# A convolution and squared-ReLU MLP layer on one core: five staging places for the spilled operands, their transfers issued by ScalarE

## The reference, cut to what matters

```python
h = rmsnorm(x, mix_norm[0])
b_gate, c_gate, v = jnp.split(h @ w_in, 3, axis=-1)      # 2048 -> 3 x 2048
u = c_gate * v
y = (b_gate * causal_conv3(u, conv_w)) @ w_out
x = x + y
h2 = rmsnorm(x, mlp_norm[0])
a = jax.nn.relu(h2 @ mlp_w1)                             # 2048 -> 8192
x = x + (a * a) @ mlp_w2                                 # 8192 -> 2048
```

## Time and profile before

| what | value |
|---|---|
| median of three runs | 2052.66 us |
| the profiled execution | 2047.96 us |
| its span, first to last instruction | 2046.2 us |
| TensorE busy (matmuls, pipelined) | 1978.9 us, 97% |
| VectorE busy | 1481.7 us, 72% |
| ScalarE busy | 851.3 us, 42% |
| GpSimd busy | 75.6 us, 4% |
| spills: 112 transfers of 512 KB from GpSimd's queue | median 7.0 us from issue to landing |

### The profile page before, as it was taken

The page is one execution under the profiler, slowest core; times in us unless marked ns, Lnnn a source line. Parts: engine busy times, 40 slices in busy tenths (PEclk is TensorE's granted clock), DMA queues, the critical chain, the costliest instruction groups (busy, mean ns, idle before and its releaser), DMA issues. The chain is left out here.

```text
span 2046.2 us, 22931 instructions
## 1 busy us (share of the span) xinstructions
PE 1978.9 (97%) x8778; PEld 1623.0 (79%) x8778; DVE 1481.7 (72%) x1368; ACT 851.3 (42%) x1002; POOL 75.6 (4%) x146
## 2 busy tenths in 40 slices
PE   8999999999999999999998999998999999999999
PEld 7888888888887877777777777777788888888887
DVE  6345363353535499879897988989888979978878
ACT  6222222222234465555545555554444433433332
POOL 0000000000000110100101010010000000000000
PEclk9999999999999999999999999999999999999999
DMA  5322222222223544757667476769889878878783
GB/s 186 118 88 103 103 82 103 102 89 95 100 98 123 196 185 165 280 211 305 242 237 276 176 274 236 285 236 367 324 318 379 330 304 325 322 308 323 273 318 134
DMA packets 98317, 445.92 MB, mean 218 GB/s; under 512 B 10800, under 2 KB 10800, under 8 KB 73776
## 3 DMA queue, kind: packets, MB, share of 16 engines
q1 hardware_dynamic: 78944, 375.42, 49.4%
q0 software_dynamic: 19136, 69.21, 8.4%
q10 hardware_dynamic: 144, 0.04, 0.0%
HBM read 371.24 MB, written 73.40 MB: 217 GB/s over the span
## 5 line engine op out<-in xcount | busy, mean ns | idle before, releaser
L1073 PE MATMUL pair<-ring,act 128*128 128x512 f32 x5376 | 1246.8, 392 | 28.5 <-DVE ring L788 18.3
L1073 PEld LDWEIGHTS pair<-ring,act 128*128 128x128 f32 x5376 | 1009.3, 189 | 251.9 <-issue 39.9
L451 ACT ACTIVATE ring<-raw 128x1024 fp32r<-128x1024 f32 x448 | 466.1, 1056 | 582.6 <-PE pair L1073 350.3
L788 DVE TENSOR_TENSOR ring<-raw,ring 128x1024 fp32r<-128x1024 f32 x448 | 540.3, 1221 | 122.2 <-ACT ring L451 120.6
L590 DVE TENSOR_TENSOR w_lo<-w_raw,w_hi 128x512 fp32r<-128x512 f32 x256 | 175.7, 692 | 348.4 <-ACT w_hi L374 343.2
L374 ACT ACTIVATE w_hi<-w_raw 128x512 fp32r<-128x512 f32 x256 | 161.4, 631 | 474.4 <-PE pair L978 471.8
L978 PE MATMUL pair<-h_hi,w_lo 128*128 128x512 f32 x764 | 297.8, 390 | 0.0
L978 PE MATMUL pair<-h_hi,w_hi 128*128 128x512 f32 x764 | 297.2, 389 | 0.0
L978 PE MATMUL pair<-h_lo,w_hi 128*128 128x512 f32 x764 | 297.2, 389 | 0.0
L783 DVE TENSOR_TENSOR raw<-raw 128x2048 f32<-128x2048 f32 x128 | 292.8, 2288 | 5.6
L978 PEld LDWEIGHTS pair<-h_hi,w_lo 128*128 128x128 f32 x764 | 143.4, 188 | 30.6 <-issue 0.8
(11 more groups left out here) (78 smaller groups left out, 750.6 us busy)
## 6 DMA issues: line engine op xcount, KB each, us to landing
raw<-in_mlp SPq DMA_DIRECT2D x128, 1024.0 KB, 7.6
act<-spill SPq DMA_DIRECT2D x224, 512.0 KB, 6.3
w_raw<-in_weights SPq DMA_DIRECT2D x63, 1024.0 KB, 4.9
spill<-stage POOLq DMA_DIRECT2D x112, 512.0 KB, 7.0
act<-act_kept SPq DMA_DIRECT2D x84, 512.0 KB, 7.6
act_kept<-act POOLq DMA_DIRECT2D x12, 512.0 KB, 6.3
mixed<-turned POOLq DMA_DIRECT2D x16, 256.0 KB, 2.9
x<-mixed SPq DMA_DIRECT2D x8, 512.0 KB, 12.7
```

The lines of the kernel that those rows point to most:

```text
L451: nc.scalar.activation(ring[g % RING][:, 0], raw[:, r, 2 * (s % 2):2 * (s % 2) + 2, :], ACT.Copy).then_inc(hi_ready, 1)
L788: nc.vector.tensor_tensor(ring[g % RING][:, 1], raw[:, RAW_OF[s // 2], 2 * (s % 2):2 * (s % 2) + 2, :], ring[g % RING][:, 0].bitcast(F32), ...
L1073: mm = nc.tensor.matmul(bank, stationary, moving, start=(opens and k == 0 and n == 0), stop=(closes and k == NT - 1 and n == 2))
```

## The change

The staging places become five (four at RESID + 16 to 32 KB, the fifth at TMP). The order of the spills and the slots in which they are split and formed change. Each pair of transfers is issued by ScalarE, in the slot after its split, behind that slot's other work, instead of by GpSimd. To make room, the sum for the first product moves to U_PAD (over quad L12) and that for L22 to H_LO + 28 KB (over quad L21), and the waits of `copy_product` and `copy_first` change with them; the waits for `turn_out` at v = 0 remain only before the copy of the fourth product. Other places in RESID are renumbered.

```diff
-SPILLS = (L11, L12, L22, S1, S3, S2, S4)
+SPILLS = (L11, L22, L12, S1, S3, S2, S4)
-SPLIT_AT = {(0, 5): 0, (0, 8): 1, (0, 9): 2, (0, 11): 3, (0, 13): 4, (1, 1): 5, (1, 3): 6}
-FORM_AT = {(0, 10): (0, 1), (0, 12): (2,), (1, 2): (3,)}
+SPLIT_AT = {(0, 4): 0, (0, 6): 1, (0, 8): 2, (0, 10): 3, (0, 12): 4, (1, 0): 5, (1, 3): 6}
+FORM_AT = {(0, 9): (0, 1), (0, 12): (2,), (1, 1): (3,)}
+STAGES = 5
...
-        sums = [at(f"sum{n}", RESID + 4 * KB * n, [P, 2, BW]) for n in range(6)]
-        q_first, q_s1, q_s2, q_s3, q_s4, q_l22 = sums
-        second_s1 = at("second_s1", RESID, [P, NT, HALF])
+        q_s1, q_s2, q_s3, q_s4 = (at(f"sum{n}", RESID + 4 * KB * n, [P, 2, BW]) for n in range(4))
+        q_first = at("sum_first", U_PAD, [P, 2, BW])
+        q_l22 = at("sum_l22", H_LO + 28 * KB, [P, 2, BW])
+        second_s1 = at("second_s1", RESID + 16 * KB, [P, NT, HALF])
...
-        stage = [at("stage0", RESID + 24 * KB, [P, NT, HALF], F32R), at("stage1", RESID + 28 * KB, [P, NT, HALF], F32R),
-                 at("stage2", TMP, [P, NT, HALF], F32R)]
+        stage = [at(f"stage{i}", a, [P, NT, HALF], F32R)
+                 for i, a in enumerate([RESID + (16 + 4 * i) * KB for i in range(4)] + [TMP])]
...
@@ gpsimd
-            def put_spill(c, n):
-                for half in range(2):
-                    w = 2 * (NPROD * c + n) + half
-                    pool.wait_ge((stage_hi, stage_lo)[half], NPROD * c + n + 1)
-                    pool.dma_start(spill[c, SPILLS[n], half], stage[w % 3][:].bitcast(F32)).then_inc(spilled[w % 3], 16)
...
-            for c in range(NC):
-                for n in range(NPROD):
-                    put_spill(c, n)
@@ scalar, copy_product(v, i)
-                if q == 0:
-                    act.wait_ge(turned, KT)
-                    act.wait_ge(turn_out, 16 * KT)
-                elif i in (0, 3, 4):
-                    act.wait_ge(quad_turned, 4 * (q - 1) + {0: 2, 3: 3, 4: 4}[i])
+                if i == 4:
+                    if q == 0:
+                        act.wait_ge(act_lo_ready, NPROD + SECOND.index(S3) + 1)
+                    else:
+                        act.wait_ge(stage_lo, NPROD * (q - 1) + SPILLS.index(S3) + 1)
+                elif q == 0:
+                    act.wait_ge(turned, 3 * NT)
+                    if i == 3:
+                        act.wait_ge(turn_out, 16 * KT)
+                elif i in (0, 3):
+                    act.wait_ge(quad_turned, 4 * (q - 1) + {0: 2, 3: 3}[i])
@@ copy_first(q)
-                    act.wait_ge(quad_turned, 4 * (q - 1) + 1)
+                    act.wait_ge(stage_lo, NPROD * q)
                 else:
-                    act.wait_ge(act_lo_ready, NPROD + SECOND.index(S2) + 1)
+                    act.wait_ge(act_lo_ready, NPROD + SECOND.index(S4) + 1)
@@ new on scalar
+            def put_spill(c, n):
+                for half in range(2):
+                    w = 2 * (NPROD * c + n) + half
+                    act.wait_ge((stage_hi, stage_lo)[half], NPROD * c + n + 1)
+                    act.dma_start(spill[c, SPILLS[n], half],
+                                  stage[w % STAGES][:].bitcast(F32)).then_inc(spilled[w % STAGES], 16)
...
                     if 2 <= v < UP and (v % 2, s) in SPLIT_AT:
                         split_z_hi(q - 1, SPLIT_AT[v % 2, s])
+                    if 2 <= v < UP and (v % 2, s - 1) in SPLIT_AT:
+                        put_spill(q - 1, SPLIT_AT[v % 2, s - 1])
                     if v >= UP and (v - UP, s) in LATE:
                         split_z_hi(NC - 1, LATE[v - UP, s])
+                    if v >= UP and (v - UP, s - 1) in LATE:
+                        put_spill(NC - 1, LATE[v - UP, s - 1])
```

More of the change, by code:

```diff
@@ L123, in conv_mlp_layer @@
         quad = {"L11": quads1[:, 0], "L21": quads1[:, 1], "L12": quads2[:, 0], "L22": quads2[:, 1]}
-        sums = [at(f"sum{n}", RESID + 4 * KB * n, [P, 2, BW]) for n in range(6)]
-        q_first, q_s1, q_s2, q_s3, q_s4, q_l22 = sums
-        second_s1 = at("second_s1", RESID, [P, NT, HALF])
-        turned_out = [at("turned0", RSTD, [P, BW])] + [at(f"turned{i + 1}", RESID + (16 + 2 * i) * KB, [P, BW])
-                                                        for i in range(4)]
-        stage = [at("stage0", RESID + 24 * KB, [P, NT, HALF], F32R), at("stage1", RESID + 28 * KB, [P, NT, HALF], F32R),
-                 at("stage2", TMP, [P, NT, HALF], F32R)]
+        q_s1, q_s2, q_s3, q_s4 = (at(f"sum{n}", RESID + 4 * KB * n, [P, 2, BW]) for n in range(4))
+        q_first = at("sum_first", U_PAD, [P, 2, BW])
+        q_l22 = at("sum_l22", H_LO + 28 * KB, [P, 2, BW])
+        second_s1 = at("second_s1", RESID + 16 * KB, [P, NT, HALF])
+        turned_out = [at("turned0", RSTD, [P, BW])] + [at(f"turned{i + 1}", RESID + a * KB, [P, BW])
+                                                        for i, a in enumerate((12, 14, 20, 22))]
+        stage = [at(f"stage{i}", a, [P, NT, HALF], F32R)
+                 for i, a in enumerate([RESID + (16 + 4 * i) * KB for i in range(4)] + [TMP])]
         acts1 = [at(f"act{j}", H_HI + 8 * KB * j, [P, 2, NT, HALF], F32R) for j in range(NPROD)]
@@ L138, in conv_mlp_layer @@
         x11, x21, x22, x12 = (at(f"x{q}", Z_LO + 8 * KB * n, [P, NP, 2, BW]) for n, q in enumerate(("11", "21", "22", "12")))
-        sum_s1 = [at("sum_s1_0", RESID + 8 * KB, [P, 2, BW]), at("sum_s1_1", RESID + 12 * KB, [P, 2, BW])]
-        sum_s2 = [at("sum_s2_0", RESID, [P, 2, BW]), at("sum_s2_1", RESID + 4 * KB, [P, 2, BW])]
+        sum_s1 = [at("sum_s1_0", RESID + 4 * KB, [P, 2, BW]), at("sum_s1_1", RESID + 8 * KB, [P, 2, BW])]
+        sum_s2 = [at("sum_s2_0", RESID, [P, 2, BW]), at("sum_s2_1", RESID + 12 * KB, [P, 2, BW])]
         pairs = [ctx.enter_context(nc.psum_tensor(f"pair{i}", [P, 2, BW], F32)) for i in range(NT)]
@@ L188, in conv_mlp_layer @@
         stage_lo = sem("stage_lo")
-        spilled = [sem(f"spilled{i}") for i in range(3)]
+        spilled = [sem(f"spilled{i}") for i in range(STAGES)]
         raw_turn_in = [sem(f"raw_turn_in{i}") for i in range(4)]
@@ L210, in spills_done @@
             n = 2 * NPROD * (c + 1)
-            for i in range(3):
-                eng.wait_ge(spilled[i], 16 * ((n + 2 - i) // 3))
+            for i in range(STAGES):
+                eng.wait_ge(spilled[i], 16 * ((n + STAGES - 1 - i) // STAGES))
         def product_done(eng, v, j):
@@ L491, in square_quad @@
                                      pairs[1][:].rearrange("p a t -> p (a t)"), ACT.Square).then_inc(quad_ready, 1)
+            def put_spill(c, n):
[4 more added lines that the diff above has]
+                                  stage[w % STAGES][:].bitcast(F32)).then_inc(spilled[w % STAGES], 16)
             def split_z_hi(c, n):
                 w = 2 * (NPROD * c + n)
-                act.wait_ge(quad_ready, 4 * c + {0: 1, 1: 3, 2: 2}.get(n, 4))
+                act.wait_ge(quad_ready, 4 * c + {0: 1, 1: 2, 2: 3}.get(n, 4))
                 if n in FORMED:
                     act.wait_ge(z_formed, 4 * c + FORMED[n])
-                if w >= 3:
-                    act.wait_ge(spilled[w % 3], 16 * (w // 3))
-                nc.scalar.activation(stage[w % 3][:], quad[HOLDS[SPILLS[n]]], ACT.Copy).then_inc(stage_hi, 1)
+                if w >= STAGES:
+                    act.wait_ge(spilled[w % STAGES], 16 * (w // STAGES))
+                nc.scalar.activation(stage[w % STAGES][:], quad[HOLDS[SPILLS[n]]], ACT.Copy).then_inc(stage_hi, 1)
             act.dma_start(cols[:], cols_dram).then_inc(cols_in, 16)
@@ L672, in first_act_form @@
             def first_act_form(f):
-                o, a, b, op, split = (("L22", "L21", "L22", ALU.add, 3), ("L21", "L11", "L21", ALU.subtract, 1),
+                o, a, b, op, split = (("L22", "L21", "L22", ALU.add, 2), ("L21", "L11", "L21", ALU.subtract, 1),
                                       ("L22", "L22", "L11", ALU.subtract, 4),
-                                      ("L12", "L12", "L22", ALU.subtract, 6))[f]
+                                      ("L12", "L12", "L22", ALU.subtract, 3))[f]
                 if f == 0:
@@ L726, in split_z_lo @@
                 dve.wait_ge(stage_hi, NPROD * c + n + 1)
-                if w + 1 >= 3:
-                    dve.wait_ge(spilled[(w + 1) % 3], 16 * ((w + 1) // 3))
+                if w + 1 >= STAGES:
+                    dve.wait_ge(spilled[(w + 1) % STAGES], 16 * ((w + 1) // STAGES))
                     dve.wait_ge(stage_lo, NPROD * c + n)
-                nc.vector.tensor_tensor(stage[(w + 1) % 3][:], quad[HOLDS[SPILLS[n]]], stage[w % 3][:].bitcast(F32),
+                nc.vector.tensor_tensor(stage[(w + 1) % STAGES][:], quad[HOLDS[SPILLS[n]]], stage[w % STAGES][:].bitcast(F32),
                                         ALU.subtract).then_inc(stage_lo, 1)
```

## The result

The changed kernel takes 2019.38 us in the median of four runs (2018.71 to 2020.46), against 2053.61 us for the kernel before, run beside it (2051.59 to 2058.87): ratio 0.983, 95% interval 0.9811 to 0.9849. The prediction was 2023 us within 2006 to 2044. The profiled execution took 2018.99 us, 29.0 us less than the one before; the medians lie 34.2 us apart.

What follows compares the result with a forecast made beforehand. TensorE, busy 97% of the span, bounds the kernel, so only its stops can be won. Terms -17.0 - 9.0 - 6.4 + 7.0 + 0 - 2.1 - 2.0 = -29.5 us; from the 2052.66 median, 2023 us, range 2006 to 2044.

Steps and rivals of the forecast that it cites:

- ring stops in the chunks: TensorE's twelve stops for the ring's low part from VectorE, outside v = 0, would go: -17.0 us.
- slot-12 stops: TensorE's "issue" stops at slot 12, one per each of seven chunks, from VectorE's lateness, would go: -9.0 us.
- cost of a stop beyond its idle time: Each TensorE stop costs 0.29 us besides its idle time; removing 12 + 7 + 3 stops gives -6.4 us.
- residue of late places: Staging places still freed late at slots 10 to 14, charged at 1.0 us a chunk: +7.0 us.
- quad stops: TensorE's waits for quads: up to 1.0 us longer stops in seven chunks, taken as offset by earlier VectorE: 0.
- v = 0 and 1: TensorE's stops in the first two turns, 0.78, 0.57 and 0.74 us, would go: -2.1 us.
- Part 2: First split at slot 4: staging copy lengthens the 2.81 us stop by up to 1.0, VectorE's earlier start cancels it: 0.
- part 5: TensorE's granted clock: dips after spill stops go, a longer quad stop may add one: -2.0 us, between -8 and +6.
- Part 3: Transfer issue on ScalarE: 0.43 us each, 6.0 us per chunk, hidden by 0.8 us at the fourth quad, elsewhere by the lead.
- the slower one: ScalarE becomes the gate if its issues last as long as SyncE's longest, 1.81 us: 2057 to 2091 us, chance 0.09.
- the wait would come back elsewhere: Landings of 11 us against 8.2 keep the slot-12 stops, quad stop grows 1.0 us: say 2046 us, chance 0.16.
- The full gain of 43 us: No late places remain and TensorE's clock stays up: -43 us, 2010 us, chance 0.10.

Runs made afterwards that it cites:

- The run with slot 5: Changed kernel with the first split moved back from slot 4 to slot 5, behind the square: 2007.33 us, ratio 0.9784.
- the early squares: Changed kernel with ScalarE's squares of the second and third quad moved to slots 3 and 5: 1981.85 us, ratio 0.9659.
- the third, with the old staging: Kernel before (three places, old slots, GpSimd issuing) with only the second and third quad's squares moved earlier: 2024.25 us, ratio 0.9879.

## Why the prediction was right

**The mechanism** was as told: late places, late VectorE, stops of TensorE. The table sets the terms against what the profiles show.

| term | predicted | measured | from |
|---|---|---|---|
| ring stops in the chunks | -17.0 | -17.0 | 0.5 us left, at v = 0 |
| slot-12 stops | -9.0 | -9.0 | 0.8 us left, at v = 1 |
| cost of a stop beyond its idle time | -6.4 | -7.8 | 38 stops became 11; 27 x 0.29 |
| residue of late places | +7.0 | 0 | no wait for transfers |
| quad stops | 0 | +4.1 | 29.2 - 25.1 |
| v = 0 and 1 | -2.1 | -0.8 | 0.78 + 0.57 + 0.74 became 0.53 + 0.79 |
| clock | -2.0 | +3.9 | 0.007 x 2017.3 = 14.1 against 10.2 |
| sum | -29.5 | -26.6 | the spans differ by 28.9 |

2.3 us are not accounted for; the mean clock is printed to 0.001, which is 2 us here. The third row's 0.29 us comes from one pair of rows, but the trace before bears it out: 19 of its 22 ring and slot-12 stops, which no fall of the clock follows, cost 0.25 to 0.30 us beyond their idle time (the way from six matmuls before to six behind, less twelve times 0.2266 and the idle time). For a stop of 0.34 us at the second quad it is 0.19.

The sum was made for the profiled execution, and 29.5 against 29.0 us looks closer than the forecast was. The medians lie 34.2 us apart, since the profiled execution of the kernel before was a quick one; its executions have clocks from 0.991 to 0.997, which is 12 us of TensorE's time between the ends.

**Two terms were mis-sized** and partly hid each other, the residue by -7 us, the quad stops and the clock by +10; that the sum came out so near is luck. The residue of 7.0 us was charged because three slots, 8.2 us, lay between the two landings in the earlier trace rows. The median landing did grow, from 7.0 to 8.8 us, and the longest to 13.7, but nobody waited; the run with four places and the one with the later issue show how near this was. The median stayed just under the 9 us that I had named as a sign of being wrong. Part 2 was right that the staging copy enters the chain (0.94 us longer) but wrong that VectorE's earlier start makes up for it: against the first quad's transposes T1 started at 1308.33 - 1309.89 = -1.56 us, where it was about -1.0 before, so half a microsecond, not one. Even that did not reach the third quad: the lead went into the 0.3 us stop at the second quad, which is gone in all chunks but the first, and T2 begins at -0.04 us against the second quad's transposes where it began at +0.03. So the stop grew by 0.9 us. The run with slot 5 prices this part at 12 us, more than the idle time, because of part 5: I expected the clock to gain 2 us, and it lost 4. With the early squares it is 1.000.

**Part 3** looked for the cost of the issue in the wrong place. The issue took 0.326 us, below the 0.43 taken, and the fourth quad's transposes never stopped. The new wait of ScalarE for the low part, which I had called one slot old when it comes, is 0.5 us once a chunk, and VectorE is 0.4 us later from there on to T2; this is also, in small, the sign that I had named, VectorE waiting for ScalarE behind the issues (0.33 us). The lock that the Trainium skill describes (Perfetto Trace Analysis, "DMA Instruction — HWDGE (DVE, Sync)") would have made issues longer with two engines at it. The trace speaks against it: 29 of the 112 issues overlap in time with one of SyncE's, and 27 of these last 0.33 to 0.35 us, like most of the rest. The other two (0.544 and 1.157 us) could be it, but an issue of 0.977 us overlaps with none of SyncE's.

**Of the rivals**, the slower one's condition, 1.81 us per issue, did not occur. That the wait would come back elsewhere is what three and four places do. The full gain of 43 us did not come, since the quad stops grew and the clock went the other way.

## What to carry to other kernels

When an engine waits for a buffer, count in slots from the issue of the transfer to the next use of its place and compare with the landing; here two slots were too few, three just enough, and only an execution shows the margin. Follow the chain of the largest remaining stop instruction by instruction: it was nothing but the order of two squares on ScalarE, behind a wait that they did not need. Moving them gained 26 us in the kernel before and 37.5 in the changed one, where some 12 of these undo what the early split had added. Where an engine computes and also issues transfers, look at the semaphore wait in front of the issue: half a microsecond of it, once a chunk, was worth 5 us or more here. Before a step is moved ahead of others on an in-order engine, look at which of those the bounding engine waits for.

## What the runs showed of the hardware

**An issue runs beside the engine's own work.** In the rows of the changed kernel above, the transfer is issued from 1321.77 to 1322.10 while ScalarE's activation of 1321.65 is still running, and the next activation starts at 1322.59 without a gap. In the chunks of the changed kernel every wait of ScalarE's in the list names an engine that it waits for, so issues of 0.33 us show no cost to its compute above the 0.2 us from which the list counts; what costs is a semaphore wait in front of them. With twice as many issues there are ten stops with nobody named, 6.2 us.

**The clock does not go by the length of the stop alone.** The windows of two kernels, the first (five places, old slots, GpSimd) with stops of 2.81 us at the quads, the second (three places, new slots, ScalarE) with 3.76:

```profile
1150.00:1160.00 10.00, 7.19 (x32) 5.96 (x31) 7.93 (x6) 7.06 (x8) 0.62 (x2) 0.83 0.13 52
```

```profile
1070.00:1080.00 10.00, 6.24 (x36) 5.13 (x35) 7.93 (x6) 7.63 (x9) 0.00 (x0) 1.00 0.27 107
```

In the first the granted clock dipped to 1.2 GHz at all eight third quads, though each stopped TensorE for only 2.8 us; in the second at four of eight, with longer stops. It is not a property of the kernel either: the profiled execution of the second has a mean clock of 0.996 and takes 2033.9 us, its three others have 0.989 to 0.991 and take 2039.4 to 2042.6. A dip takes 0.17 of the 10 us of the first window, 1.7 us. Without these stops two kernels had no dip in the turns and a mean of 1.000 in all eight executions; the profile of the third, with the old staging, has one dip, behind a ring stop of 2.52 us. What decides between equal stops stays open.

**With five places a transfer took longer than with three.** The median from issue to landing was 6.7 to 7.3 us in the four profiles with three places, 7.9 with four, and 7.6 to 10.3 in the eight with five and whole transfers: 8.7 to 8.9 in the new slots, 9.7 and 10.3 in the old ones, and 7.6 to 7.7 with the early squares or with the issue two slots later. The sizes are equal. That more transfers are in flight at once would explain it, but the spread among the kernels with five places shows that it is not the number alone. The queue made no difference (8.8 and 8.7, 7.6 and 7.7).
